# Three chunks of an output projection moved ahead of a wait, and rotary copies moved from ScalarE to SyncE

## What is computed

```python
# latent attention, 16 heads
q_rope = apply_rope(q_rope, cos, sin) * ATTN_SCALE            # 32 rotary columns a head
q_lat = einsum('bshn,chn->bshc', q_nope, w_uk) * ATTN_SCALE
s = einsum('bqhc,bkc->bhqk', q_lat, c_kv) + einsum('bqhr,bkr->bhqk', q_rope, k_rope)
p = softmax(s)

# hybrid layer: two attentions, each projected up and gated, then merged
y_a = merge_heads(o_a) * silu(sb_z)
y_b = o_b * silu(n_z)                                         # o_b: sparse attention, 512 columns
merged = sigmoid(gate_a) * (y_a @ w_up_a) + sigmoid(gate_b) * (y_b @ w_up_b)
x = x + merged @ w_out
```

## Time and profile before

| | before |
|---|---|
| time, median of 3 runs | 3025.47 us (3022.55 to 3027.57) |
| profiled execution, its time | 3016.31 us |
| profiled execution, span of its instructions | 3014.5 us |
| busy: PE, PEld, DVE, ACT, POOL | 2870.3, 2508.2, 2144.1, 1432.9, 409.3 us |
| granted TensorE clock, mean | 0.984 of full speed |

### The profile page before, as it was taken

One profiled execution on the slowest core, in us unless ns is written; L12 is line 12 of the kernel. 1 busy time (PEld: TensorE's weight loads), 2 busy tenths in 40 slices (PEclk: granted clock), 3 DMA queues, 4 the chain that ended last, 5 costly groups with the idle time before them and its releaser, 6 DMA issues.

```text
span 3014.5 us, 43783 instructions
## 1 busy us (share of the span) xinstructions
PE 2870.3 (95%) x17258; PEld 2508.2 (83%) x17258; DVE 2144.1 (71%) x3229; ACT 1432.9 (48%) x2363; POOL 409.3 (14%) x303
## 2 busy tenths in 40 slices
PE   7999989999999999789999999999899999999999
PEld 6999879998889988667789988787787777877777
DVE  6888678888688876789587855377677532876763
ACT  4455234555245552466455532373655434655552
POOL 1100102000101000100300000312300233041003
PEclk9999999999999999999999999999999999999999
DMA  6665632665636645100235432302211232032113
GB/s 234 218 207 169 221 133 71 204 203 176 208 119 214 213 161 189 61 15 11 81 110 167 147 103 93 119 29 70 98 50 57 91 108 89 15 98 78 57 50 112
DMA packets 100252, 365.35 MB, mean 121 GB/s; under 512 B 11600, under 2 KB 12368, under 8 KB 99408
## 3 DMA queue, kind: packets, MB, share of 16 engines
q1 hardware_dynamic: 70784, 254.63, 24.2%
q0 software_dynamic: 25280, 92.29, 11.3%
q10 hardware_dynamic: 3984, 15.64, 1.5%
HBM read 354.12 MB, written 6.29 MB: 120 GB/s over the span
## 4 chain that ended last, share of the span: by engine, by line
PE 74%; DVE 15%; ACT 4%; issue 4%; DMA 2%; POOL 1%; ACTq 1%; SPq 0%; DVEq 0%; POOLq 0%
PE psum L482 56%; PE psum L2578 7%; PE psum L1476 2%; PE psum L1443 2%; DVE w_lo L455 2%; PE psum L2522 2%; ACT w_hi L440 1%; DVE a_lo L1063 1%; PE psum L539 1%; DMA raw<-stream_in 1%; DVE tb L606 1%; PE psum L848 1%; PE psum L550 1%; DMA ada_first<-ada_in 1%; DVE h_lo L615 1%
## 5 line engine op out<-in xcount | busy, mean ns | idle before, releaser
L440 ACT ACTIVATE w_hi<-raw 128x1024 fp32r<-128x1024 f32 x353 | 368.2, 1053 | 348.5 <-DMA raw<-stream_in 212.0
L461 POOL TENSOR_TENSOR w_lo<-raw,w_hi 128x1024 fp32r<-128x1024 f32 x115 | 285.4, 2487 | 1345.5 <-ACT w_hi L440 1345.3
L482 PE MATMUL psum<-h_hi,w_hi 128*128 128x256 f32 (+1 forms) x1632 | 367.7, 336 | 26.2 <-DVE h_lo L615 8.9
L482 PE MATMUL psum<-h_hi,w_lo 128*128 128x256 f32 (+1 forms) x1632 | 354.9, 328 | 0.0
L482 PE MATMUL psum<-h_lo,w_hi 128*128 128x256 f32 (+1 forms) x1632 | 352.8, 326 | 0.0
L455 DVE TENSOR_TENSOR w_lo<-raw,w_hi 128x1024 fp32r<-128x1024 f32 x238 | 289.8, 1220 | 74.7 <-ACT w_hi L440 74.6
L440 ACT ACTIVATE w_hi<-xr 128x1024 fp32r<-128x1024 f32 x200 | 211.4, 1057 | 227.6 <-DVE xr L1146 78.1
L482 PEld LDWEIGHTS psum<-h_hi,w_hi 128*128 128x128 f32 x1632 | 259.8, 191 | 68.3 <-DVE h_lo L615 14.5
L482 PE MATMUL psum<-t_hi,w_hi 128*128 128x256 f32 (+1 forms) x1536 | 284.9, 300 | 7.2 <-DVE a_lo L1063 5.4
L482 PE MATMUL psum<-t_hi,w_lo 128*128 128x256 f32 (+1 forms) x1536 | 281.8, 298 | 0.0
L482 PEld LDWEIGHTS psum<-h_hi,w_lo 128*128 128x128 f32 x1632 | 258.6, 189 | 27.6
(11 more groups left out here) (503 smaller groups left out, 5568.0 us busy)
## 6 DMA issues: line engine op xcount, KB each, us to landing
raw<-stream_in SPq DMA_DIRECT2D x353, 512.0 KB, 3.5
ada_raw<-ada_in POOLq DMA_DIRECT2D x128, 512.0 KB, 5.7
xr<-stream_in SPq DMA_DIRECT2D x120, 512.0 KB, 4.5
xr<-stream_in POOLq DMA_DIRECT2D x40, 512.0 KB, 5.6
ada_first<-ada_in POOLq DMA_DIRECT2D x4, 1024.0 KB, 17.2
ada_first<-ada_in SPq DMA_DIRECT2D x4, 1024.0 KB, 22.4
x_held<-X ACTq DMA_DIRECT2D x2, 2048.0 KB, 7.7
X<-x_held ACTq DMA_DIRECT2D x2, 2048.0 KB, 7.7
```

What stands on the lines that cost most here:

```text
L440: act.activation(w_hi[:, u % RING], tile, ACT.Copy, scale=-1.0 if u in negated else 1.0).then_inc(hi_ready, 1)
L461: pool.tensor_tensor(w_lo[:, u % RING], source[u][0], w_hi[:, u % RING].bitcast(F32), ALU.subtract).then_inc(lo_ready, 1)
L482: mm = pe.matmul(dst, w[wi], m[mi], start=(first and n == 0), stop=(last and n == total - 1), skip_group_check=skip)
```

## The change

Two places are edited. In the latent attention `high` no longer issues the rotary copies; a new function `rope_sp` issues the same 32 copies on SyncE, in order of pairs, between the weight fetches of units `wo + 1` and `wo + 2` (the second and third units of that layer's output projection). It waits for the last rotated halves before the first copy. ScalarE's part for kind "q" moves from the step (0, 2), between its exponential and the turned weights' high half, to the end of step (0, 1), behind that step's high half and ahead of the exponential of (0, 2).

In the hybrid layers one of the eight up products, the first that falls on PSUM bank 0, is begun before the wait for y_b's last chunk with chunks 0 to 2, and finished with chunk 3 when its turn comes. It is the third product in the first hybrid layer and the first in the second.

```diff
@@ high(act, kind, p)
-                if kind == "q":
-                    for t in (2 * p, 2 * p + 1):
-                        src, to = ROPE_ROWS[t % 4]
-                        for a, b in ((qt_hi, qr_hi), (qt_lo, qr_lo)):
-                            act.dma_start(a[to:to + 32, t % 4].bitcast(F32), b[src:src + 32, t // 4].bitcast(F32)).then_inc(rope_moved[p % 2], 16)
@@ run(eng, who, k, phase)
                     else:
                         kind = {(0, 2): "q", (0, 3): "k", (1, 1): "v"}.get(at_)
+                        if who == "act":
+                            kind = None if kind == "q" else kind
+                            if at_ == (0, 1) and phase == 1 and p + 1 < 8:
+                                todo.append(("q", p + 1))
@@ new function
+        def rope_sp(sp, L):
+
+            sp.wait_ge(part_hi.sem, part_hi.at((L, "rot", 3)))
+            sp.wait_ge(h_ready.sem, h_ready.at((L, "rot", 3)))
+            for p in range(HEADS // 2):
+                if p >= 2:
+                    sp.wait_ge(scores.sem, scores.at((L, 4 * (2 * p - 3) + 3)))
+                for t in (2 * p, 2 * p + 1):
+                    src, to = ROPE_ROWS[t % 4]
+                    for a, b in ((qt_hi, qr_hi), (qt_lo, qr_lo)):
+                        sp.dma_start(a[to:to + 32, t % 4].bitcast(F32), b[src:src + 32, t // 4].bitcast(F32)).then_inc(rope_moved[p % 2], 16)
@@ hybrid_pe(pe, l)
+            early = -g % 4
+            pe.wait_ge(evac.sem, evac.at(("g", own[L, "ng", 6])))
+            pe.wait_ge(lo_ready, u + early // 2 + 1)
+
+            def merged(n, chunks, first, last):
+                blocks_of = [4 * (n % 2) + c for c in chunks]
+                return three_passes(pe, bank(g + n), unit_blocks(u + n // 2, blocks_of), chunks_of(nq_hi, nq_lo, chunks),
+                                    first=first, last=last, skip=True)
+            merged(early, range(3), True, False)
             pe.wait_ge(h_ready.sem, h_ready.at((L, "yb", 3)))
             pe.wait_ge(gated.sem, gated.at((L, len(MERGE) - 1)))
             for n in range(NC):
                 pe.wait_ge(lo_ready, u + n // 2 + 1)
-                free_bank(pe, g + n)
-                mm = three_passes(pe, bank(g + n), unit_blocks(u + n // 2, range(4 * (n % 2), 4 * (n % 2) + 4)),
-                                  chunks_of(nq_hi, nq_lo, range(4)))
+                if n == early:
+                    mm = merged(n, [3], False, True)
+                else:
+                    free_bank(pe, g + n)
+                    mm = merged(n, range(4), True, True)
@@ block.sync
             for u in range(own["mla", "u"], own["ffn3", "u"]):
+                if u == own["mla", "wo"] + 2:
+                    rope_sp(sp, "mla")
                 fetch(sp, u)
```

## The result

| | before | changed |
|---|---|---|
| median of the runs of this measurement, us | 3024.01 (3020.71 to 3027.57) | 3002.78 (2997.49 to 3006.45) |
| ratio | 1 | 0.9928 [0.9908, 0.9948] |
| profiled execution, us | 3016.31 | 3006.45 |
| its span, us | 3014.5 | 3004.6 |
| its mean granted clock | 0.984 | 0.985 |

What follows compares the result with a forecast made beforehand. TensorE held 74% of the chain, with VectorE setting the pace in the attention loop. Seam 9.9 plus loop 6.5 gave 16.4 us saved, 3025.5 - 16.4 = 3009.1 us, range 3004 to 3018.

Steps and rivals of the forecast that it cites:

- The seam: Between sparse attention and output projection in both hybrid layers: nine matmuls fill PE's wait, full clock stays; 9.9 us saved.
- The late DVE: Behind the seam, DVE's last low half was put 0.2 us late for PE in one layer; 0.3 us taken off.
- The new block of 2 us at the first sum: Behind the seam, DVE's first sum falls into POOL's 2.37 us operation, costing 2 us of DVE's lead.
- the walk: Steps through the seam's eight products, DVE blocked beside POOL: last low half at 2396.2 and 2397.0, PE wanting it at 2396.8.
- The loop: Latent attention's softmax loop over eight pairs of heads: 4.3 + 1.0 + 1.2 = 6.5 us saved, bounds 0 and 11.6.
- The start: Start of the attention loop: first scores come 1.0 to 2.0 us earlier, counted as 1.2 us saved.
- the first pair: First pair inside the attention loop: its 1.7 us wait for qt_hi becomes about 0.7, saving 1.0 us.
- The six pairs behind it: Six attention-loop pairs: DVE's 1.32 us wait goes, a 0.66 us wait comes, net 0.72 us each; 4.3 us saved.
- (a): Attention loop: ACT issues no rotary copies, four a pair at 0.61 us each; costed together with the loop's other edits.
- (b): Attention loop: qt_hi is computed ahead of the exponential, starting at 1331.64 instead of 1333.73.
- (c): Attention loop: the exponential slips behind qt_hi, from 1331.62 to 1332.85, giving DVE's reciprocal a new wait of 0.66 us.
- the difference carries over: Whole kernel: PE is again the chain behind both places, so 16.4 us come off the 3025.5 us median.

Runs made afterwards that it cites:

- Experiment 3: Kernel before plus nine extra matmuls with unread sums in PE's wait at each seam, all 288 still behind it: 3015.81 us, ratio 0.9981.
- experiment 11: Changed kernel with qt_hi back behind the exponential, two products begun early per seam, and DVE instead of POOL making four weight units' low halves: 2999.16 us, 0.9914.
- experiment 4: The changed kernel measured once more, unaltered, beside new runs of the kernel before: 3004.67 us, ratio 0.9947 to before.
- the three later groups: Runs of the unchanged kernel before, taken beside the three groups of follow-up experiments: medians 3021.07, 3022.13 and 3021.69 us.
- experiment 7: Kernel before with only qt_hi moved ahead of the exponential; ACT still issues the copies, now behind the exponential; seams as before: 3012.88 us, 0.9974.
- experiment 1: Changed kernel without the early products: only the attention loop's edits (copies on SP, qt_hi's new place), seams as before: 3011.95 us, 0.9974.
- experiment 6: Kernel before with only the rotary copies moved to SP; qt_hi stays behind the exponential, seams as before: 3005.25 us, 0.9953.

## Why the prediction came out as it did

**The seam: right, and nearly right in size.** Nine matmuls in the wait, full clock behind it, 64.3 us for the rest where 64.0 had been forecast; 9.2 us in all against 9.9 (5.2 + 5.1 - 0.3 is in fact 10.0). Experiment 3 shows the cause apart: 2.8 us a seam from the clock, 2.07 from moved work. Both the forecast and the 9.2 lean on the one trace of before; against the mean of the eight untouched seams (68.5 us) the gain is 7.9. The late DVE was there as well: PE waited once for mg_lo, in layer 0:

```profile
PE psum L482 <- DVE mg_lo_six L3312: 0.4, 1, 0.4
```

0.2 us had been walked out. The new block of 2 us at the first sum did not come: in layer 0 the sum took 0.69 us, since POOL's operation had ended 1.1 us before it, and in layer 1 it took 1.54. The Trainium skill, page "SBUF — State Buffer", section "Who interferes with whom", has the exclusion of DVE and GpSimd that the walk contained. The trace agrees: three of DVE's low halves took 2.12 us in the chain above instead of 0.69, beside POOL operations of 2.56 us, and in experiment 11, which takes POOL's four operations away, PE no longer waits.

**The loop: right in mechanism, with one term left out.** Forecast a new wait of 0.66 and a period of 19.7; measured 0.59 and 19.71. The start gained 1.4 (forecast 1.2). The sum, 6.5 against 7.7, was short at the first pair: the chain's step at 1308.13 moved to 1304.52, 3.6 us, of which 0.24 came from ahead of the loop, where the start and the first pair had 1.2 + 1.0 = 2.2. So the first pair gave 2.0 us for the 1.0 forecast. Its term priced only the wait for qt_hi; it put the clock at nothing, while the half-clock stretch behind the wait of 2.03 us (in the section on the result) goes with the wait. The six pairs behind it gave the 4.3 forecast.

**What the working didn't separate.** Edits (a), (b) and (c) were costed as one. Taken alone, (a) lets qt_hi follow the exponential at once, at 1332.4 by the earlier trace rows, ahead of DVE's need; (b) and (c) then have nothing to gain and 0.7 us to lose. That sum could have been made from the earlier trace rows. It would have shown that the period could fall to 19.0, close to PE's own work. It doesn't change the forecast's number, but it is the larger finding.

**The step that failed** is the last one of the sum: "the difference carries over: 3025.5 - 16.4", with "the median itself moves 2.5 us": the mis-sized term is the level of before that it starts from, 3025.5 us where more runs show 3021.6. The difference did carry over: nine runs of the changed kernel have a median of 3004.23 us, 59 runs of the kernel before one of 3021.64, 17.4 us apart (17.0 with only the five changed runs of experiment 4). But the 3025.47 of three runs lies 3.8 us above the median of the 59. These run from 3012.4 to 3029.1 us with a standard deviation of 3.9, and medians of three drawn from them scatter by 2.6 either way. Against the true level the forecast would have been 3021.6 - 16.4 = 3005.2; the true difference is 1.0 more than forecast, and the four runs of the first measurement fell another 1.5 below their own level. These are the 6.3 us of the miss: 3.8, 1.0 and 1.5. The last is luck of the draw. The first may be luck too, for the scatter is enough to give it. But a fourth run of before left the median of the first measurement at 3024.0, while the medians of the three later groups lie within 1.1 us of each other; a level that was higher at that time isn't excluded. The profiled execution at 3016.31, 0.3% below the median of the three, had been a hint that their median was high, and it was passed over. The range was cut at 3004 on the fast side as if only the mechanisms could err there.

## What to carry to other kernels

When PE waits 3 us before a run of matmuls, look for products whose first operands are ready: what they save is their own time and, if they leave little enough idle (1.4 to 1.5 us here), the half-clock stretch behind as well, and even discarded work gets the second. When a change removes an obstacle and also moves the step behind it, cost each edit alone: here the removal had made the step early enough, and the move only delayed another. Where runs scatter by as much as a term of the sum, anchor on more than three runs, give the level's own uncertainty to the range on both sides, and read each place in the trace.

## What the runs showed of the hardware

- Runs of one kernel differ with the clock they are granted. Over the 59 runs of before the mean time was 3016.2 us at a mean granted clock of 0.985 (5 runs), 3019.0 at 0.984 (25), 3023.1 at 0.983 (10), 3022.8 at 0.982 (12) and 3024.9 at 0.981 (7). The traces show half-clock stretches at different places in different executions; why stays open.
- Four DMA issues by ACT for each pair, behind its last urgent activation, were free (19.71 us a pair in experiment 7, 19.70 without them in experiment 1), while taking the same four away from ahead of one was worth 12.0 us over the loop, its start included (experiment 6).
- SP took 0.59 us (median) to issue one of these 32-row copies, nearly as long as ACT with 0.61, and not the 0.33 of its weight fetches: between these two engines the price went with the transfer.
- The same wait doesn't always cost the same. Behind 3.5 us of idle time at a seam, 288 matmuls took from 67.93 to 69.19 us (eight seams in four traces), where they took 66.4 at full clock. Behind 2.83 us, in one execution, 285 took 67.10 at the first seam and 68.43 at the second, where 0.2305 us each would be 65.7.
- Full clock was held over 1.43 to 1.46 us of idle time in every trace with such a wait at the loop's start or at a seam; after 2.03 to 2.13 us at the loop's start it fell in all four.
